# Forget-gate mixer: the finest level in the diagonal's product, a denominator ahead of its numerator, and three first-chunk steps instead of two

## What is computed

```python
def hgrn step(S, (qc, kc, vc, fc)):              # one chunk, 4 heads of 128
    Bc = cumsum(fc)                              # log decay, per token and feature
    A = einsum('tk,sk,tsk->ts', qc, kc, exp(Bc[t] - Bc[s]))   # for s <= t
    o = (qc * exp(Bc)) S + A vc
    S = exp(Bc[-1]) * S + (kc * exp(Bc[-1] - Bc))^T vc
def mlstm step(C, n, m):
    num = P vc + w_st * (qc C);  den = sum(P) + w_st * (qc n)
    h = num / max(|den|, exp(-mt))
```

## Time and profile before

| | |
|---|---|
| median of 3 runs | 2270.25 us (2268.61 to 2273.75) |
| profiled execution | 2264.96 us, span of the trace 2263.1 us |
| mean granted clock of the tensor engine | 0.986 of full |
| tensor engine (PE) busy | 2185.4 us, 97% |
| vector engine (DVE) busy | 958.1 us, 42% |
| scalar engine (ACT) busy | 758.8 us, 34% |
| Pool engine busy | 577.8 us, 26% |
| evacuation of a dense group (line 419) | 458 ns each, x177 |

### The profile page before, as it was taken

How to read it: one execution, slowest core, us unless ns; L and a number is a source line. 1 busy time by engine, 2 the same in 40 slices (tenths; PEclk the granted TensorE clock), 3 DMA queues, 4 the chain that set the end, 5 groups by cost and what they waited for, 6 DMA issues and landing times.

```text
span 2263.1 us, 36330 instructions
## 1 busy us (share of the span) xinstructions
PE 2185.4 (97%) x13818; PEld 2121.1 (94%) x13818; DVE 958.1 (42%) x1512; ACT 758.8 (34%) x1334; POOL 577.8 (26%) x375
## 2 busy tenths in 40 slices
PE   7999999999999999999999799999999999999997
PEld 6999999999799999899998788999999999999997
DVE  5888233324556572244443366352222222222225
ACT  5555323233355563233331333232212212122132
POOL 1439522323121112212212222222221211212221
PEclk9999999999999999999998999999999999999999
DMA  4223646442324323246431754311110111111112
GB/s 175 59 84 96 193 129 175 132 125 77 105 90 137 119 72 121 88 148 185 139 110 43 237 164 142 114 38 38 47 61 28 51 46 37 60 32 51 51 33 91
DMA packets 191538, 222.09 MB, mean 98 GB/s; under 512 B 38670, under 2 KB 146226, under 8 KB 191334
## 3 DMA queue, kind: packets, MB, share of 16 engines
q1 hardware_dynamic: 168476, 181.91, 26.6%
q10 hardware_dynamic: 22986, 39.13, 4.8%
HBM read 162.22 MB, written 58.77 MB: 98 GB/s over the span
## 4 chain that ended last, share of the span: by engine, by line
PE 80%; issue 7%; DVE 7%; POOL 3%; DMA 2%; ACT 1%; SPq 0%; ACTq 0%; DVEq 0%; POOLq 0%
PE D L400 68%; DVE m_rd L2008 1%; POOL w_lo L381 1%; POOL b_t L705 1%; POOL b_u L702 1%; DVE u_x L514 1%; PE MM L839 1%; PE MM L1781 1%; PE MM L1204 1%; DVE acc L2307 1%; DMA proj<-stage 0%; PE M L839 0%; PE M L2157 0%; DVE xn_lo L2438 0%; PE M L2125 0%
## 5 line engine op out<-in xcount | busy, mean ns | idle before, releaser
L400 PE MATMUL D<-xn_hi,w_hi 128*128 128x352 f32 x1992 | 668.0, 335 | 10.4 <-POOL w_lo L381 3.7
L381 POOL TENSOR_TENSOR w_lo<-w_raw,w_hi 128x1024 fp32r<-128x1024 f32 (+1 forms) x169 | 353.7, 2093 | 1265.7 <-ACT w_hi L375 1265.7
L400 PE MATMUL D<-xn_lo,w_hi 128*128 128x352 f32 x1992 | 647.3, 325 | 0.0
L400 PE MATMUL D<-xn_hi,w_lo 128*128 128x352 f32 x1992 | 646.8, 325 | 0.0
L400 PEld LDWEIGHTS D<-xn_hi,w_hi 128*128 128x128 f32 x1992 | 378.5, 190 | 29.8 <-issue 14.6
L400 PEld LDWEIGHTS D<-xn_lo,w_hi 128*128 128x128 f32 x1992 | 378.5, 190 | 4.7 <-issue 3.8
L400 PEld LDWEIGHTS D<-xn_hi,w_lo 128*128 128x128 f32 x1992 | 378.2, 190 | 0.0
L375 ACT ACTIVATE w_hi<-w_raw 128x1024 fp32r<-128x1024 f32 (+1 forms) x169 | 147.5, 873 | 365.9 <-PE D L400 337.7
L400 PE MATMUL D<-h_lo,w_hi 128*128 128x352 f32 x768 | 248.1, 323 | 0.0
L400 PE MATMUL D<-z_lo,w_hi 128*128 128x352 f32 x768 | 247.9, 323 | 0.0
L400 PE MATMUL D<-z_hi,w_lo 128*128 128x352 f32 x768 | 247.8, 323 | 0.0
(11 more groups left out here) (505 smaller groups left out, 2817.6 us busy)
## 6 DMA issues: line engine op xcount, KB each, us to landing
w_raw<-in_w_proj SPq DMA_DIRECT2D x73, 512.0 KB, 3.9
proj<-stage ACTq DMA_DIRECT2D x60, 528.0 KB, 2.9
w_raw<-in_w_half SPq DMA_DIRECT2D x72, 256.0 KB, 2.6
stage<-proj SPq DMA_DIRECT2D x24, 528.0 KB, 3.6
w_raw<-in_w_full SPq DMA_DIRECT2D x24, 512.0 KB, 3.5
d_bc<-rowd SPq DMA_DIRECT2D x32, 256.0 KB, 5.9
m_in<-proj SPq DMA_DIRECT2D x32, 256.0 KB, 3.7
f_w<-in_w_full SPq DMA_DIRECT2D x16, 512.0 KB, 3.5
```

What stands on the lines that cost most here:

```text
L381: nc.gpsimd.tensor_tensor(w_lo[t.slot][:, 0:kt, :], raw(t)[0][:, 0:kt * P].rearrange("p (k m) -> p k m", m=P), w_hi[t.slot][:, 0:kt, :].bi ...
L400: last = nc.tensor.matmul(D[b][:, 0:GN], w[t.slot][:, k, :], x[:, k, cols], start=(k == 0 and n == 0), stop=(k == kt - 1 and n == 2))
```

## The change

For the prompt's chunks, level 0 leaves the chain of levels. With half width 1 a block is a pair of neighbours, and the whole decay from key to query can be put on the query's side; the key is then the plain key that the diagonal uses. `ql0` (64 columns a head) is written behind each head's 128 plain queries in `g_sl`, which grows to 192 columns a head, and one product for each head gives diagonal and level 0 together, 192 columns wide, in banks M[0] and M[1] (now one tensor `MB`). `dk0` and `kl0` are no longer made. On the vector engine the predicated copy of level 0 (`cp0`) follows the diagonal's copy at once, ahead of the next chunk's clamp; the other three stay where they were. The remaining levels move by one place in the banks, so `top` comes after level 3. The product now waits for `ql0`, and the scalar copies and the key transposes wait for `cp0`.

In the mLSTM the denominator's product comes ahead of the numerator's, line 2010 waits for the numerator, and `ML_SLOTS` goes from `[3, 3, 4, 3, 3, 2]` to `[3, 3, 3, 3, 3, 3]`. In `hgrn_first` the scalar engine does only the sigmoids at `between(1)`; the logarithms and the key (`"forget", 2`) move to `between(2)`, which is moved up to stand right behind the copy at line 1716, and the exponential of `dq` becomes `between(3)` where `between(2)` was.

```diff
-            g_sl = arena(a, "g_sl", [P, 2 * N4])
+            g_sl = arena(a, "g_sl", [P, 3 * N4])
...
+        MB = ctx.enter_context(nc.psum_tensor("MB", [P, 2 * 512], F32))
+        M01 = [MB[:, i * 512:(i + 1) * 512] for i in range(2)]
...
+        LQ = CH + CH // 2
...
+        def near(lo, hi):
+            two = MB[:, :].rearrange("p (a f) -> p a f", f=512)[:, :, 0:2 * LQ]
+            return two.rearrange("p a (h c) -> p a h c", c=LQ)[:, :, :, lo:hi]
...
+            first_key = 0 if sample else 1
...
-                    for j in range(L)[:4] if part == 4 else range(L)[4:]:
+                    for j in range(first_key, L)[:4] if part == 4 else range(first_key, L)[4:]:
...
+                        q = q_of(g_sl).rearrange("p h (b c) -> p h b c", c=2 * hf)[:, :, :, hf:2 * hf]
+                        to = q_odd(g_sl).unsqueeze(3) if j == 0 else by_head(g_ql[:, j * HF:(j + 1) * HF])
+                        eng.tensor_tensor(to, q, by_head(g_dq[:, j * HF:(j + 1) * HF]), ALU.mult).then_inc(*dve_.step(f"ql{j}"))
...
-                    for j, hf in enumerate(halves):
+                    for j, hf in list(enumerate(halves))[first_key:]:
                         eng.tensor_tensor(cb(g_dk, hf, j * HF), blk(g_b, hf)[:, :, hf - 1:hf].to_broadcast([P, C4 // (2 * hf), hf]),
...
-            for part in {"dve": [(0,), (6, 1), (2,), (3,)], "act": [(0,), (1, 2), (3,)]}[kind][at]:
+            for part in {"dve": [(0,), (6, 1), (2,), (3,)], "act": [(0,), ("sigmoids",), ("forget", 2), (3,)]}[kind][at]:
...
-                return M[1 + j // 2][rows, j % 2 * HF:(j % 2 + 1) * HF]
+                return M[2 + (j - 1) // 2][rows, (j - 1) % 2 * HF:((j - 1) % 2 + 1) * HF]
...
-                    eng.wait_ge(*dve_.after("at", n))
+                    eng.wait_ge(*dve_.after("cp0", n))
                     eng.wait_ge(*pe_.after("top", n))
...
+                    eng.tensor_tensor(g_at[:, :].rearrange("p (a h n) -> p a h n", a=2, n=N), near(0, CH),
+                                      cst[:, CC_ID:CC_ID + N].unsqueeze(1).unsqueeze(1).to_broadcast([P, 2, 2, N]), ALU.mult).then_inc(*dve_.step("at"))
+                    eng.wait_ge(*dve_.after("at", n))
+                    eng.sem_inc(hg_levels, 1)
+                    eng.copy_predicated(g_at[:, :].rearrange("p (a h b c) -> p a h b c", a=2, h=2, c=2)[:, :, :, :, 1],
+                                        cst[:, msk:msk + HF].bitcast(mybir.dt.uint32).rearrange("p (a h b) -> p a h b", a=2, h=2), near(CH, LQ)).then_inc(*dve_.step("cp0"))
                 prep(0)
                 prep(6)
...
                 for j, hf in enumerate(halves[:4]):
+                    if j == 0 and not sample:
+                        continue
...
+                    eng.wait_ge(*df.after("ql0", n))
+                    for h in range(H):
+                        i = eng.matmul(near(0, LQ)[:, h // 2, h % 2, :], hn(g_k)[:, h, :], g_sl[:, h * LQ:(h + 1) * LQ], start=True, stop=True)
                 i.then_inc(*pe_.step("diag"))
...
-                for j in reversed(range(L)):
+                for j in reversed(range(last_level, L)):
...
-                    if j in (0, 4):
-                        i.then_inc(*pe_.step("lev" if j == 0 else "top"))
-                eng.wait_ge(*dve_.after("at", n))
+                    if j in (last_level, 4 if sample else 3):
+                        i.then_inc(*pe_.step("lev" if j == last_level else "top"))
+                eng.wait_ge(*dve_.after("at" if sample else "cp0", n))
...
                 eng.activation(sq(B.t), sq(M[5]), ACT.Copy).then_inc(*act_.step("tr"))
+                between(2)
                 slot()
...
-                between(2)
+                between(3)
...
-        ml_pe = steps("ml_pe", "vt kq kt num den kv ss", credit=1)
+        ml_pe = steps("ml_pe", "vt kq kt den num kv ss", credit=1)
...
+                if not sample:
+                    eng.wait_ge(*pe_.after("num", n))
                 eng.tensor_tensor(m_h[:, 0:C4], M[1][:, 0:C4], m_rd[:, 0:C4], ALU.mult).then_inc(*dve_.step("h"))
...
+                else:
+                    i = eng.matmul(M[2][:, :], ones, m_qn[:, :], start=True, stop=True)
+                    i.then_inc(*pe_.step("den"))
                 for h in range(H):
...
-        ROW_SLOTS, ML_SLOTS = [9, 2, 4, 3], [3, 3, 4, 3, 3, 2]
+        ROW_SLOTS, ML_SLOTS = [9, 2, 4, 3], [3, 3, 3, 3, 3, 3]
```

More of the change, by code:

```diff
@@ L205, in build @@
             g_e2 = arena(a, "g_e2", [P, 2, N4])
-            arena(a, "g_gap", [P, N4])
             g_in = arena(a, "g_in", [P, 3 * N4])
@@ L766, in levels @@
             return " ".join(f"{name}{j}" for j in range(n))
-        hf_act = steps("hf_act", f"{PREP_ACT} {levels('kl', 7)} eb ed")
-        hf_dve = steps("hf_dve", f"{PREP_DVE} {levels('dq', 7)} bk {levels('dk', 7)} dl {levels('ql', 7)} qe")
+        hf_act = steps("hf_act", f"{PREP_ACT} {levels('kl', 7)[4:]} eb ed")
+        hf_dve = steps("hf_dve", f"{PREP_DVE} {levels('dq', 7)} bk {levels('dk', 7)[4:]} dl {levels('ql', 7)} qe")
         hg_act = steps("hg_act", f"vt {levels('c', 7)} kt sq rl rr", credit=1)
@@ L877, in hgrn_prep @@
                     eng.activation(g_lf[:, 0:C4], g_sg[:, 2 * C4:3 * C4], ACT.Exp, scale=-1.0).then_inc(*act_.step("sf"))
+                if part in (1, "forget"):
                     eng.wait_ge(*act_.after("sf", n, ahead))
@@ L1047, in level @@
             def level(j, rows=slice(0, N)):
-                return M[1 + j // 2][rows, j % 2 * HF:(j % 2 + 1) * HF]
+                if sample:
+                    return M[1 + j // 2][rows, j % 2 * HF:(j % 2 + 1) * HF]
+                return M[2 + (j - 1) // 2][rows, (j - 1) % 2 * HF:((j - 1) % 2 + 1) * HF]
             if kind == "sp":
@@ L1195, in hgrn @@
                 eng.wait_ge(*af.after("k", n))
-                for h in range(H):
-                    i = eng.matmul(M[0][0:N, h * N:(h + 1) * N], hn(g_k)[:, h, :], hn(g_sl)[:, h, :], start=True, stop=True)
+                last_level = 0 if sample else 1
+                if sample:
+                    for h in range(H):
+                        i = eng.matmul(M[0][0:N, h * N:(h + 1) * N], hn(g_k)[:, h, :], hn(g_sl)[:, h, :], start=True, stop=True)
+                else:
+                    eng.wait_ge(*df.after("ql0", n))
+                    for h in range(H):
+                        i = eng.matmul(near(0, LQ)[:, h // 2, h % 2, :], hn(g_k)[:, h, :], g_sl[:, h * LQ:(h + 1) * LQ], start=True, stop=True)
                 i.then_inc(*pe_.step("diag"))
@@ L2141, in mlstm @@
                     i = eng.matmul(M[2][:, 0:C4], ones, m_qn[:, 0:C4], start=False, stop=True)
-                else:
-                    i = eng.matmul(M[2][:, :], ones, m_qn[:, :], start=True, stop=True)
-                i.then_inc(*pe_.step("den"))
-                if sample:
+                    i.then_inc(*pe_.step("den"))
                     for h in range(H):
```

39 lines of the change are left out of this document (27 added, 12 removed).

## The result

The changed kernel takes **2259.08 us** (median of five runs, 2255.67 to 2260.74) against 2270.66 us for the kernel before on the same chip (2268.61 to 2273.75): a ratio of 0.9946, 95% interval 0.9933 to 0.9958. That is 11.6 us less (9.5 to 15.2 by the interval); the forecast was 6.9 less, and 2263.3 us on the median. Its profiled execution has a span of 2257.4 us and a mean granted clock of 0.986, like that of before (2263.1 us, 0.986): in this pair the gain is only 5.7 us.

What follows compares the result with a forecast made beforehand. The tensor engine, busy 97% of the span, was taken to bound the kernel; terms +3.2 (forget-gate chunks), -5.9 (mLSTM chunks) and -4.2 (delta-rule sample part) sum to -6.9 us, 2263.3 us on the median, range 2256 to 2271 us.

Steps and rivals of the forecast that it cites:

- The sign: Whole kernel: faster, -6.9 us in sum; chance 0.63 of being faster by more than 4.5 us.
- the chosen case: Whole kernel: the main forecast of -6.9 us, 2263.3 us, given chance 0.60 against the three rivals.
- the five terms: Forget-gate chunks: six +5.0 us, first -0.9, last -0.9; eight mLSTM chunks -5.9; delta-rule sample part -4.2.
- part 2: Eight mLSTM chunks: denominator ahead and slots evened remove the wait at the sum of squares, -5.9 us.
- part 3: Delta-rule sample part: first-chunk steps in three cut the 2.84 us wait and the low clock behind it, -4.2 us.
- last chunk: Last forget-gate chunk: tensor engine's -0.49 us counts and its wait of about 0.45 goes, -0.9 us.
- rival (b): Six forget-gate chunks: waits of about 1.6 us make the clock fall, +15 us, total +8.1, 2278.4 us; chance 0.12.
- part 1: Eight forget-gate chunks: finest level joins the diagonal; tensor work saved turns into waiting, +3.2 us in all.
- Rival (a): Forget-gate chunks: the chain does not bind, the saved load is kept, -3.9 us; total -14.0, 2256.2 us; chance 0.12.
- Rival (c): First forget-gate chunk: its DMA wait takes back the delta-rule sample part's gain; total -2.7, 2267.6 us; chance 0.16.
- The term of six chunks: Forget-gate chunks 2 to 7: later clamp, activations and key copy delay the state product 0.83 us each, +5.0 us.
- The term of the first chunk: First forget-gate chunk: the new copy hides in the clamp's 3.54 us DMA wait, one copy fewer at the end, -0.9 us.

Runs made afterwards that it cites:

- cp0_late: The kernel after, with only the moved predicated copy put behind the next chunk's clamp; 2251.27 us, ratio 0.9911.
- part 1 alone: The kernel before with only the finest level joined to the diagonal's product, without the mLSTM and `hgrn_first` edits; 2266.42 us, ratio 0.9984.
- part 3 alone: The kernel before with only the first chunk's logarithms and key moved behind the next copy; 2267.01 us, ratio 0.9977.
- gin_early: The kernel before, with the forget-gate inputs' three DMA requests ahead of the weight tile's load in SP's order; 2262.24 us, ratio 0.9968.
- clamp_first_before: The kernel before, with the next chunk's clamp put ahead of the diagonal's masked copy on the vector engine; 2270.35 us, ratio 1.0001.
- part 2 alone: The kernel before with only the mLSTM denominator ahead of the numerator and `ML_SLOTS` evened; 2262.03 us, ratio 0.9963.

## Why the prediction was right or wrong

**Right, and for the reasons given, though the largest gain was not among them.** The sign, the range and the chosen case hold, and would hold by stages without the first chunk's surprise (-8.1); by stages, three of the five terms came out within 0.1 us (part 2: -5.9; part 3: -4.1 for -4.2; last chunk: -1.0 for -0.9). Clamp, activations, copies, then the key copy as what is late next, is what the trace after shows, and cp0_late shows the moved copy as the cause. The clock stayed full after 1.3 us of waiting, so rival (b) fell: seven waits of 1.3 and no chunk with a lower clock, and the same again with part 1 alone. It was nearer than that sounds: one wait of 1.6 us, at 74 us of the program, has half clock for 3.4 us behind it in five of the fourteen kernels and full clock in the rest. Rival (a) fell in the order chosen. Rival (c) is true of part 3 alone, 0.9 us, and not of the change.

**The term of six chunks, mis-sized: +5.0 forecast (0.83 each), +3.8 measured.** The shift of the activations is 1.11, not 1.30: the diagonal is later by 0.40 and the copy by 0.73 + 0.16, but the clamp, which waits for nothing on its own engine, starts at 674.17, 0.20 before that copy's end (674.37). I had charged a gap ahead of it as ahead of a dependent copy. The slack ahead of the state product was 0.58 rather than 0.47: it starts 0.05 us behind the key copy, its weight load at the same moment, where I had put 0.11 between the two. 1.11 - 0.58 = 0.53, which is what the start of the state product lost in the chunk of the rows (12.52 us behind the diagonal before, 13.05 after). Then the next dense matmul starts 0.91 us behind it instead of 0.81, which was not forecast.

The rest lies in the kernel before, whose chunks were not alike. Its clamp stood 1.70 us behind the diagonal in three of the six chunks; in the chunk of the rows it was 1.79 and in the last two 1.90 and 1.97, as the inputs landed late there too (vector engine, seventh chunk, before):

```profile
825.02 0.96 DVE L920 TENSOR_SCALAR g_x<-g_in 128x1536 f32<-128x1536 f32 x1 [0.18 <-DMA g_in<-proj]
```

Those chunks took 35.4, 35.5 and 35.6 us, the others 35.3. Behind the moved copy the clamp never waits, and all take 36.03 to 36.05. Against an undisturbed chunk the loss is 0.74 us, 4.4 for six; the 0.6 that lateness had cost come off that. The row from which I took the wait of 0.69 was one of the late ones; its neighbours have 0.59.

On the two pages weighed: the 48 level records of 64 columns take 5.30 us, 0.11 each, which bears out the cost by weight load that the Trainium skill gives in "TensorE: Matmul & The Clock Gate", section "LDWEIGHTS (loading the stationary operand)". The 0.1625 us at 192 columns goes by the moving columns (0.43 x 192 / 512 = 0.16). The gap of 0.16 between the masked copy and the dependent copy is there again, where the Trainium skill, "VectorE: DVE Perf Modes", section "The DRAIN you can't avoid", says that the semaphore costs nothing extra.

**The term of the first chunk, missed: -0.9 forecast, -5.8 measured.** The prediction let the new copy hide in the wait for the inputs and kept that wait as it was. It saw the DMA as fixed relative to the tensor engine. The runs show instead that its request follows the Pool engine's product, that part 1 shortens that one by 0.93 us, that the transfer then takes 2.1 us less, and that with a stall of 1.3 instead of 4.0 the 3.4 us are gone too that the low clock had cost in this trace. I had used that clock row for a price in rival (b) and never asked what it would be worth to lose the stall. gin_early shows that the transfer's time is enough for all of it. Why the transfer itself is shorter (6.0 for 8.1 us) stays open. The scalar engine's next store of a projection group is requested 1.10 us ahead of the diagonal in both kernels and `g_v` 0.33 behind it, so a transfer requested 0.94 sooner has more of its time without them; that fits and was not tried alone.

**The sum.** Forecast -6.9; by stages -13.0; by medians -11.6. The missed term of -4.9 and the loss that is smaller by 1.2 make up the whole difference of 6.1 between forecast and stages. That the profiled pair gained only 5.7 is the low clock in the sample parts, as above; that 5.7 is near the forecast of 6.9 is luck. About 3.4 of the -5.8 and 1.7 of the -4.1 are clock behind a stall, which other kernels with the same stalls didn't all pay, so each of these two terms could come out 1 to 3 us smaller in another pair of executions.

## What to carry to other kernels

When an instruction is moved on an engine with little load, look at what stands behind it in that engine's order, not at the engine's share: 0.9 us on a vector engine busy 42% of the time cost more than the 0.49 that the tensor engine saved, and one place further down the chunks were no longer than before. When a wait is ended by a DMA, follow the DMA back to its request and to what that stands behind; it moves with work that seems to have nothing to do with it. Price a stall together with the clock that may follow it: the 4.0 us one cost 7.4 in one kernel's trace and 5.7 in another's.

## What was unexpected of the hardware

- Pool and vector engine seem to slow one another down, and which comes first can turn: the 128x1024 product of line 381 takes mostly 2.4 us on Pool elsewhere, 4.40 or 3.47 beside the vector engine here, and the vector engine's 128x512 product takes 0.69 or 2.90. All eight kernels without part 1 had 4.40 and 0.69, all six with it 3.47 and 2.90.
- A predicated copy of 128x256 costs by its pattern and not by where it reads: half width 2 takes 0.74 us from M[1] before and 0.75 from the MM banks after, while half widths 4 and 8 take 1.01 together.
- The same stall is not followed by the same clock. Behind the 4.0 us stall of the first chunk it was at half for 6.8 us in the kernel before and in clamp_first_before, for 3.4 us with part 2 alone. Behind the 2.84 us wait in the sample part it was at half for 3.4 us in seven kernels, and stayed full in clamp_first_before (row below). After the waits of 1.2 to 1.4 us in the forget-gate chunks it stayed full each time.

```profile
558.20:561.60 3.40, 3.40 (x29) 2.85 (x30) 0.68 (x1) 0.74 (x3) 0.00 (x0) 1.00 0.02 5
```
